# An attention stage whose query blocks are taken in the order 4, 0, 5, 1, 6, 2, 7, 3

## The reference

```python
qb = (q * scale).reshape(b, nb, Q_BLOCK, ATTN_HEADS, 2, ATTN_HEAD_DIM)   # Q_BLOCK = 128, nb = 8
def block(args):                                       # one block of 128 queries, all heads
    q_blk, i = args
    sc = einsum('bhcqd,bhckd->bhcqk', q_blk, kt)       # two maps c per head
    sc = where(k_pos[None, :] <= q_pos[:, None], sc, -inf)
    p = softmax(sc, axis=-1)
    p_diff = p[:, :, 0] - lam * p[:, :, 1]
    return einsum('bhqk,bhkv->bhqv', p_diff, vt)
o = rms_norm(o, subln_g) * (1.0 - lambda_init)
```

## Time and profile before

| | |
|---|---|
| median of 3 runs | 1843.36 us (1842.89 to 1843.89) |
| the profiled execution: its time, its span | 1842.73 us, 1841.1 us |
| PE busy over the span | 1793.0 us, 97% |
| DVE busy over the span | 1137.9 us, 62% |
| the attention, first scores to the last transposes of a difference | 135.5 us to 505 us |

### The profile page before, as it was taken

One profiled execution on the slowest core, in us unless ns is written; L12 is line 12 of the kernel. 1 busy time (PEld: TensorE's weight loads), 2 busy tenths in 40 slices (PEclk: granted clock), 3 DMA queues, 4 the chain that ended last, 5 costly groups with the idle time before them and its releaser, 6 DMA issues. The chain is left out here.

```text
span 1841.1 us, 25124 instructions
## 1 busy us (share of the span) xinstructions
PE 1793.0 (97%) x8628; PEld 1480.4 (80%) x8628; DVE 1137.9 (62%) x1786; ACT 688.4 (37%) x1351; POOL 219.5 (12%) x494
## 2 busy tenths in 40 slices
PE   6999999999999999999999999999999999999997
PEld 5887777777878888888888888888888888788885
DVE  4218888898875774541555645874555555567666
ACT  4216666666644333342221123433333333222122
POOL 2121111111110001112100112100000000000002
PEclk9999999999999999999999999999999999999999
DMA  6220111111132223327635612212222222333332
GB/s 216 92 64 27 55 59 57 58 57 57 46 138 80 76 67 104 126 81 262 217 126 171 229 57 108 86 69 74 97 68 91 80 75 96 103 127 124 125 126 92
DMA packets 123088, 187.11 MB, mean 102 GB/s; under 512 B 5936, under 2 KB 93488, under 8 KB 121984
## 3 DMA queue, kind: packets, MB, share of 16 engines
q1 hardware_dynamic: 99376, 99.36, 17.1%
q0 software_dynamic: 23344, 85.69, 12.7%
q10 hardware_dynamic: 288, 1.05, 0.2%
HBM read 136.79 MB, written 49.28 MB: 101 GB/s over the span
## 5 line engine op out<-in xcount | busy, mean ns | idle before, releaser
L2056 PE MATMUL ps<-w_d,hn 128*128 128x512 f32 x960 | 218.1, 389 | 0.0
L2122 PE MATMUL ps<-xn,ring 128*128 128x512 f32 x864 | 214.2, 398 | 1.4 <-DVE qt L1431 1.0
L2056 PEld LDWEIGHTS ps<-w_d,hn 128*128 128x128 f32 x960 | 180.2, 188 | 37.4
L2122 PEld LDWEIGHTS ps<-xn,ring 128*128 128x128 f32 x864 | 158.3, 189 | 33.1 <-issue 1.1
L2365 PE MATMUL ps<-s_op,t_op_T 128*128 128x512 f32 x720 | 170.0, 389 | 2.2 <-ACT a_copy L786 2.2
L2365 PEld LDWEIGHTS ps<-s_op,t_op_T 128*128 128x128 f32 x720 | 135.1, 188 | 30.7 <-ACT a_copy L786 2.7
L2231 PE MATMUL ps<-s_op,x_op_T 128*128 128x512 f32 x540 | 127.4, 389 | 0.0
L1996 DVE TENSOR_TENSOR ff_sum<-ff_sum,ps 128x512 f32<-128x512 f32 x128 | 87.9, 687 | 52.5 <-PE ps L2056 52.5
L2231 PEld LDWEIGHTS ps<-s_op,x_op_T 128*128 128x128 f32 x540 | 101.4, 188 | 21.0
L2365 PE MATMUL ps<-hn,t_op_B 128*128 128x512 f32 x480 | 115.1, 389 | 0.0
L2365 PEld LDWEIGHTS ps<-hn,t_op_B 128*128 128x128 f32 x480 | 90.1, 188 | 18.7
(11 more groups left out here) (221 smaller groups left out, 3199.1 us busy)
## 6 DMA issues: line engine op xcount, KB each, us to landing
pair<-in_w_gate_up_dram SPq DMA_DIRECT2D x20, 1024.0 KB, 5.1
x_pair<-in_w_in_dram SPq DMA_DIRECT2D x15, 1024.0 KB, 6.4
raw<-in_w_in_dram SPq DMA_DIRECT2D x28, 512.0 KB, 4.0
raw_down<-in_w_down_dram SPq DMA_DIRECT2D x22, 512.0 KB, 3.4
raw_down<-hf_scratch SPq DMA_DIRECT2D x22, 512.0 KB, 3.2
hf_scratch<-hf_out POOLq DMA_DIRECT2D x40, 256.0 KB, 2.3
gate_in<-gate_scratch POOLq DMA_DIRECT2D x18, 512.0 KB, 3.6
y_scratch<-y_out POOLq DMA_DIRECT2D x8, 1024.0 KB, 4.2
```

Of the source, the lines that this page charges most:

```text
L2056: last = pe.matmul(ps[:, bank, :], lhs, rhs, start=i == 0, stop=i == len(pairs) - 1)
L2122: last = pe.matmul(ps[:, proj_bank(first, half), :], ring[:, which, a, P * k:P * (k + 1)], xn[:, b, k, HALF * half:HALF * (half + 1)], sta ...
```

## The change

The block of a step is no longer its index: a table gives it. Large and small blocks alternate.

```diff
+        BLOCKS = (4, 0, 5, 1, 6, 2, 7, 3)
+        def half_of(which, turn):
+            return 1 - turn if which else turn
...
             def exps(i, c):
-                w = P * (i + 1)
+                w = P * (BLOCKS[i] + 1)
...
             def scores(par, i):
                 wait_for(pe, exp_done, t.at() * 2)
-                for chunk in range(i // 4 + 1):
-                    w = min(HALF, P * (i + 1) - HALF * chunk)
+                q = BLOCKS[i]
+                for chunk in range(q // 4 + 1):
+                    w = min(HALF, P * (q + 1) - HALF * chunk)
```

The same replacement is made in `masked`, `maximum`, `difference`, the copies of the transposes, `diff_transposed`, `weighted_values` and `y_lo`/`y_hi`. Since block 4 comes first, the second half of the queries is projected first (`half_of(1, turn)` is `1 - turn`), in the prelude of head 0 as well:

```diff
             def proj_part(which, part, first=False):
-                half, ks = part // 2, range(4 * (part % 2), 4 * (part % 2) + 4)
+                half, ks = half_of(which, part // 2), range(4 * (part % 2), 4 * (part % 2) + 4)
+                bank = proj_bank(first, part // 2)
...
                     if i == 0:
                         pe.wait_ge(proj_lo, p.at(-1))
-                    if i == 4:
-                        pe.wait_ge(proj_lo, p.at(-2))
+                    if i == 1:
+                        pe.wait_ge(proj_lo, p.at())
                     scores(par, i)
```

The two weight splits of a head move one step up, on ACT and on DVE; the split of the values stays at the fifth step:

```diff
                 if not lag:
-                    if i in (2, 6):
+                    if i in (1, 5):
                         split_next()
                     if i == 4 and not last:
                         split_v(1 - par)
                     if i % 2 == 1 and not last:
-                        proj_lo_of(1 - par, i // 4, i // 2 % 2)
+                        proj_lo_of(1 - par, i // 4, half_of(i // 4, i // 2 % 2))
```

More of the change, by code:

```diff
@@ L859, in _, with proj_hi_of @@
             t, heads_in, heads_out = Count(), Count(), Count()
-            def proj_hi_of(par, which, half, first=False):
+            def proj_hi_of(par, which, half, first=False, turn=None):
                 act.wait_ge(proj_done, p.at(1))
-                copy((kt, qt)[which][:, par, HH, HALF * half:HALF * (half + 1)], ps[:, proj_bank(first, half), :],
+                bank = proj_bank(first, half if turn is None else turn)
+                copy((kt, qt)[which][:, par, HH, HALF * half:HALF * (half + 1)], ps[:, bank, :],
                      scale=(1.0, HD ** -0.5)[which]).then_inc(proj_hi, 1)
@@ L931, in y_hi @@
                     act.wait_ge(y_free, heads_out.at())
-                transposed_hi(1, y_out[:, par, HH, P * i:P * (i + 1)].rearrange("p (k t) -> p k t", t=P), 1)
+                s = slice(P * BLOCKS[i], P * BLOCKS[i] + P)
+                transposed_hi(1, y_out[:, par, HH, s].rearrange("p (k t) -> p k t", t=P), 1)
             def split_v(par):
@@ L946, in step_of @@
                     before = (i - 1) % TT
-                    for b in range(before // 4 + 1):
-                        blocks = min(4, before + 1 - 4 * b)
+                    for b in range(BLOCKS[before] // 4 + 1):
+                        blocks = min(4, BLOCKS[before] + 1 - 4 * b)
                         transposed_hi(b, pt[:, before % 2, HH, 4 * b:4 * b + blocks, :], blocks)
@@ L978, in _ @@
             for half in range(2):
-                proj_hi_of(0, 1, half, first=True)
+                proj_hi_of(0, 1, half_of(1, half), first=True, turn=half)
             for i in range(TT):
@@ L1426, in _, with proj_lo_of @@
             t = Count()
-            def proj_lo_of(par, which, half, first=False):
+            def proj_lo_of(par, which, half, first=False, turn=None):
                 dve.wait_ge(proj_hi, p.at(1))
                 buf, s = (kt, qt)[which], slice(HALF * half, HALF * (half + 1))
-                dve.scalar_tensor_tensor(buf[:, par, LL, s], ps[:, proj_bank(first, half), :], (1.0, HD ** -0.5)[which],
+                dve.scalar_tensor_tensor(buf[:, par, LL, s], ps[:, proj_bank(first, half if turn is None else turn), :],
+                                         (1.0, HD ** -0.5)[which],
                                          buf[:, par, HH, s].bitcast(F32), ALU.mult, ALU.subtract)\
@@ L1455, in masked @@
                 dve.wait_ge(scores_done, t.at(1))
-                block = ps[:, i // 4:i // 4 + 3:2, P * (i % 4):P * (i % 4 + 1)]
+                q = BLOCKS[i]
+                block = ps[:, q // 4:q // 4 + 3:2, P * (q % 4):P * (q % 4 + 1)]
                 did(dve.tensor_tensor(block, block, mask[:, :, :], ALU.add))
@@ L1477, in y_lo @@
             def y_lo(par, i):
-                transposed_lo(1, lambda s: y_out[:, par, s, P * i:P * (i + 1)].rearrange("p (k t) -> p k t", t=P), 1)
+                cols = slice(P * BLOCKS[i], P * BLOCKS[i] + P)
+                transposed_lo(1, lambda s: y_out[:, par, s, cols].rearrange("p (k t) -> p k t", t=P), 1)
             def step_of(par, i, lag=0, first=False, last=False):
@@ L1513, in _ @@
             for half in range(2):
-                proj_lo_of(0, 1, half, first=True)
+                proj_lo_of(0, 1, half_of(1, half), first=True, turn=half)
             dve.wait_ge(mask_ready, 2)
@@ L2121, in proj_part @@
                     for a, b in PASSES:
-                        last = pe.matmul(ps[:, proj_bank(first, half), :], ring[:, which, a, P * k:P * (k + 1)],
+                        last = pe.matmul(ps[:, bank, :], ring[:, which, a, P * k:P * (k + 1)],
                                          xn[:, b, k, HALF * half:HALF * (half + 1)],
@@ L2137, in scores @@
                             rows = slice(HD * c, HD * (c + 1))
-                            last = pe.matmul(ps[:, 2 * c + chunk, 0:w], qt[rows, par, a, P * i:P * (i + 1)],
+                            last = pe.matmul(ps[:, 2 * c + chunk, 0:w], qt[rows, par, a, P * q:P * (q + 1)],
                                              kt[rows, par, b, HALF * chunk:HALF * chunk + w],
@@ L2144, in diff_transposed @@
                 pe.wait_ge(diff_ready, t.at())
-                for b in range(i // 4 + 1):
-                    blocks = min(4, i + 1 - 4 * b)
+                for b in range(BLOCKS[i] // 4 + 1):
+                    blocks = min(4, BLOCKS[i] + 1 - 4 * b)
                     transpose_rows(b, diff[:, i % 2, HALF * b:HALF * b + P * blocks], blocks)
@@ L2153, in weighted_values @@
                     heads_v.next()
-                for b in range(i // 4 + 1):
+                for b in range(BLOCKS[i] // 4 + 1):
                     pe.wait_ge(tr_free[b], tr[b].at(-newer[b]))
                 wait_for(pe, u_ready, t.at(-2))
-                for k in range(i + 1):
+                for k in range(BLOCKS[i] + 1):
                     pe.matmul(ps[:, U_BANK, 0:2 * HV], pt[:, i % 2, HH, k, :], vh[:, par, :, k, :],
-                              start=k == 0, stop=k == i, skip_group_check=True)
+                              start=k == 0, stop=k == BLOCKS[i], skip_group_check=True)
                     last = pe.matmul(ps[:, U_BANK, 0:HV], pt[:, i % 2, LL, k, :], vh[:, par, HH, k, :],
-                                     start=False, stop=k == i, skip_group_check=True)
+                                     start=False, stop=k == BLOCKS[i], skip_group_check=True)
                 last.then_inc(pv_done, 1)
@@ L2181, in step_of @@
                     diff_transposed(before)
-                    newer = (1, before // 4)
+                    newer = (1, BLOCKS[before] // 4)
                 if lag == 1:
```

11 lines of the change are left out of this document (6 added, 5 removed).

## The result

| | kernel before | changed kernel |
|---|---|---|
| median | 1843.34 us (1841.91 to 1844.84, 7 runs) | 1848.96 us (1846.97 to 1851.17, 7 runs) |
| ratio, 95% interval | | 1.0031, 1.002 to 1.0042 |
| profiled execution: time, span | 1842.73, 1841.1 | 1847.28, 1845.7 |
| head 0 | 42.04 | 44.36 |
| loop, six heads in all | 279.85 | 284.54 |

The change makes the kernel slower by 0.31%, 5.6 us. The prediction said 1846.3 us, +0.16%. The range (1840.5 to 1850.5) holds the result, and so does the forecast's own (1843.5 to 1849), by 0.04 us; "within 0.2%", which the prediction gave as its likeliest case, does not.

A forecast was written before the change was run, and what follows sets the result against it. PE is busy 97% of the span, so only its idle time in the attention, mostly waits for DVE, can move. Loop +2.6, head 0 +2.7, head 7 and end -2.4 give +2.9 us: 1846.3 us, range 1840.5 to 1850.5.

The forecast's parts named there:

- within 0.2%: Whole kernel: the forecast's case, a steady head of 46.8 to 47.2 us and a time within 0.2%; chance 0.47.
- The ring: One steady attention head, followed along whatever ends last: eight stretches summing to 46.97 us, against 46.64 before.
- S1 to M2: From the start of block 0's scores to block 5's mask: 6.46 us, DVE's side adding up to 6.5.
- the bank in step 5: PE's wait for bank 5 behind block 6's first four transposes: 1.05 us, where the kernel before has 0.56.
- the last difference: Last head's end: PE's wait for block 3's difference, 1.03 us before, would fall to 0.3.
- waits at `rsums`: Sign of being wrong: the forecast fails if waits stand at `rsums`; no size given.
- The loop's turn: DVE's next mask 1.50 us late, 1.3 absorbed by block 4's step; 0.2 us left in three of six heads.
- Head 0 and the end: First head, nothing covering block 4's chain: +2.7 us; head 7 and the end: -2.4 us.
- Rival 1: Step 5, block 6's copy on DVE needing ACT's: exponentials 0.5 us later, +3.8, 1850 us; chance 0.37 with its neighbours.
- M5 to M6: From block 2's mask to block 7's mask on DVE: 6.30 us, much other would show the prediction wrong.
- Rival 2: Large blocks' chain is DVE's own work, short copies shorten it: 1.8 us a head, 1834 us; faster cases together 0.16.
- Rival 3: Spread over a head, DVE's work fits under PE's: 2.3 us a head, 1830 us; faster cases together 0.16.

The follow-up runs named there:

- c3: Changed kernel with ACT's high half of the values' split in step 3 and DVE's low half ahead of step 4's difference: 1842.98 us, 1.0003 of the kernel before.
- b4: Changed kernel with the weight splits put back in steps 2 and 6, block order as changed: 1858.53 us, 1.0086 of the kernel before.
- a3: Changed kernel with DVE's low half of the values' split issued behind step 4's `y_lo`: 1845.96 us, 1.0016 of the kernel before.
- a2: Changed kernel with DVE's loop over heads 1 to 6 written out, other engines' loops kept: 1845.82 us, 1.0016 of the kernel before.
- d1: Kernel before with the values' split moved to step 0 of the head that uses them, POOL's load left in place: 1836.38 us, 0.9964.
- a1_again: The changed kernel measured once more, no edit: 1847.77 us, 1.0027 of the kernel before.
- b2: Kernel before with the values' split in step 0 and POOL's load behind step 3's norm, loops kept: 1836.36 us, 0.9961.
- c1: Kernel before with the weight splits in steps 1 and 5, block order as before: 1843.69 us, 0.9999.
- b1: Changed kernel with the values' split in step 0, POOL's load behind step 3's norm and DVE's loop written out: 1838.4 us, 0.9971 of the kernel before.
- a4: Changed kernel with the values' split in step 0 of the head that uses them, POOL's load left in place: 1849.42 us, 1.0037 of the kernel before.
- c2: Kernel before with only POOL's load moved behind step 3's norm, the values' split left in step 4: 1882.33 us, 1.0203.
- b3: Kernel before with the values' split in step 0, POOL's load behind step 3's norm and DVE's loop written out: 1837.24 us, 0.9961.

## Why the prediction was right, and where it was not

**The ring: right.** Steady heads are 46.95 us against 46.97 forecast, and no stretch is off by more than 0.04. The chains that the prediction named (exponentials for a large block, norm for a small one, the values' split in front of bank 5) are the ones in the trace, and c3 and b4 move the heads by what these chains give. In S1 to M2 some of that is luck: DVE's side adds up to 6.5, the prediction took 6.46 without a reason, and 6.43 came.

The waits' sizes came less well: 0.80 for the bank in step 5 against 1.05 (the split starts at 349.11 and PE goes on at 350.78, 1.67 us later as said, but the four transposes in front end, by their record, at 349.98 and cover 0.87 of it, not 0.6), about 0.15 for the last difference against 0.3 (its transposes start 0.37 us behind the `y_row` transpose at 507.37, where 0.22 is usual); the differences' 0.25 to 0.68 and the norm's 0.28 to 0.56 are near what was said (0.2 to 0.8, 0.4 to 0.7), the one of 0.28 in step 5 being below it. a3 shows a coupling that the ring had left out: what delays `sum_u` delays the norm of the next step.

One of the signs of being wrong did appear: waits at `rsums`, 28 of them, 15.8 us in all. By the prediction's own account of the order (a short copy behind a large block leaves DVE waiting for the exponentials) they had to appear. The ring had priced the stretches from a large block's mask to its difference whole, exponentials included, so their lengths held (5.02 against 5.00, 6.01 against 6.02). The sign was listed wrongly; the ring does not fall with it.

**The loop's turn: mis-sized, and the cause of the miss.** The prediction carried the 1.50 us of the earlier trace rows over as a delay of fixed length, gave block 4's step 1.3 us of room for it, and so left "0.2 us in three of six heads". Measured: the odd heads of a2, whose DVE has no turn, are 0.18 us longer than the even ones (so were those of the kernel before, 46.78 against 46.51; whose doing that is stays open; in the old order it goes when the values' split moves, d1). On top of these 47.13 us the turn costs 1.17 and 1.10 us in heads 3 and 5 of the first trace, 1.24 and 1.40 in a1_again, and nothing in head 1, which stands behind the loop's entry. The six heads together: 6 x (46.95 - 46.64) + 3 x 0.18 + 2.3 = +4.7 us, where the prediction had 2.0 + 0.6 = +2.6. The room was right: of gaps of 2.42, 2.35, 2.40 and 2.60 us on DVE (two turns in each of the two traces) 1.25, 1.25, 1.16 and 1.20 do not reach the head's length. The gap was wrong, because it is not of fixed length. In ACT's timeline, first before, then after, the high copy of `y_out` is the last thing that DVE waited for ahead of the turn:

```profile
270.98 0.28 ACT L786 ACTIVATE y_out<-ps 128x128 fp32r<-128x128 f32 x1
```

```profile
272.41 0.28 ACT L792 ACTIVATE y_out<-ps 128x128 fp32r<-128x128 f32 x1
```

From its end to DVE's next mask it is 274.33 - 271.26 = 3.07 us before and 275.76 - 272.69 = 3.07 after. In the old order DVE is behind and still has 1.5 us of work in hand when that wait is released, so only 1.50 shows, and step 0 absorbs it. In the new one DVE has caught up: 2.42 shows, of which block 4's chain absorbs about half. The rest arrives at PE in step 1:

```profile
278.88 0.55 PE L2151 MATMUL ps<-kt,qt 64*128 64x128 f32 x6 [0.16 <-ACT e_t L911]
...
280.39 0.76 PE L2075 MATMUL ps<-ident,diff 128*128 128x128 f32 x5 [0.95 <-DVE diff L1459]
```

That the turn is the cause is shown (a2). That its length counts from the last wait passed is read from eleven traces, not tried by an experiment, and what DVE's sequencer does in that time no run shows.

The Trainium skill (Advanced Engine Details and Errata, Control Flow Timing) gives a compare-and-branch about 108 ns; no row here shows a single branch. The turn of this loop costs far more than one: the same way, from ACT's copy to DVE's mask, takes 0.82 us in head 4, where there is no turn, so the turn adds 2.25 us, about 21 times that figure.

**Head 0 and the end: right in kind.** Head 0 +2.32 against +2.7; block 4's transposes wait 0.77 us for the difference in step 1, where 0.85 was said. The end -2.98 against -2.4: head 7 to its last difference's transposes takes 507.74 - 462.65 = 45.09 us (forecast 45.1 to 45.4) and the short steps behind it have a little less. The attention as a whole is then +2.32 + 4.69 - 2.98 = +4.0 us instead of +2.9.

**The rest is not shown to be the change's.** The first scores come 1.7 us earlier (133.75 against 135.47). Over the traces of all kernels here they come between 133.75 and 135.47 in no order, so this is chance. Against it stands +2.3 us behind the attention, +1.9 of it in one place of the feed-forward. PE waits there for ACT about as long as before, and in the trace of before the granted clock stays at 1.00. In that of after it falls: 12 matmuls run at the lower level, 1.2 GHz, for part of the stretch.

```profile
1583.34 3.02 PE L2365 MATMUL ps<-s_op,t_op_T 128*128 128x512 f32 x12 [2.23 <-ACT a_copy L786]
```

```profile
1586.23 4.61 PE L2378 MATMUL ps<-s_op,t_op_T 128*128 128x512 f32 x12 [2.53 <-ACT a_copy L792]
```

In b2, which has the old order, the same 12 matmuls take 4.54 us after a wait of 2.57, and c1, old order too, shows a clock of 0.97 over the same 50 us as the changed kernel. In fact the trace of before is the only one of fourteen without this fall: in the other thirteen, five of them of the old order, the 12 matmuls take 4.33 to 4.61 us after waits of 2.01 to 2.68. So the order is not needed for it; why the first trace was spared is open. From the attention's end to the span's, the six traces of the old order take 1312.1 to 1314.5 us, the eight of the new one 1312.4 to 1314.7. A hint the other way stays unexplained: the mean granted clock is 0.995 or 0.996 in all 15 runs of the changed kernel, and 0.996 or 0.997 in 62 of the 63 runs of the kernel before that were taken beside the experiments. The falls may thus be more frequent in the new order.

In the profiled runs the parts add up: -1.7 + 4.0 + 2.3 = +4.6 us of span. The medians differ by 5.6, and the interval (3.7 to 7.7 us) holds both; of these 5.6 the attention's 4.0 are placed, the other 1.6 are not. With the turn taken out, a2 stands 2.8 us above the kernel before, where the prediction had +2.9 with only 0.6 for the turn.

**The rivals.** Rival 1 (slower, 1850, for a delay of block 6's copy on DVE by ACT in step 5) came nearer in time, 1.0 us off where the forecast was 2.7 off, but by the wrong mechanism: no wait for ACT's copy stands there, and M5 to M6 is 6.27. A reader who had gone by the time alone would have believed it. Rival 2 (short copies shorten the chain) falls: DVE waits for the exponentials 28 times. Rival 3 (DVE fits under PE) falls with the 26 waits for a difference. The unasked question was the larger one: not in which order the blocks stand, but where the values' split stands. Its move is worth 1.0 us a head in the old order (b2, d1) and, with the load moved behind a norm, 0.9 to 1.1 in the new (b1 against a2); the best version keeps the old order.

## What to carry to other kernels

When an engine that is nearly saturated holds a buffer that others wait for, first move the work that stands between its last use and its release, and only then think of the order of the blocks; a filler belongs where that engine waits for another (c3: -0.69 us a head, b2: -1.0). Price a loop's turn from the last wait passed ahead of it (read from the traces here, not tried), not from the gap that the old profile shows: a change that lets the engine catch up uncovers it. A load and the work that its wait is tied to are one step; moved singly, either can block a queue (a4: DVE's wait for the norm rises from 0.56 to 1.54 us) or starve the split (c2: +39 us).

## What the hardware showed unexpectedly

- In the eleven traces with DVE's loop kept, old order and new, two turns each, DVE's first instruction behind the turn started 2.99 to 3.27 us after the end of the ACT copy that DVE had last waited for. At the head's start in the middle of the unrolled pair, with DVE just as caught up, it is 0.82 us, of which 0.15 is a wait for the scores (head 4); with the loop written out (a2) it is 0.82 at the turn's place too.
- The turn can be hidden whole: in the old order heads 3 and 5 (46.78 us) are as long as head 1 (46.77), and writing the loop out gives nothing (b3).
- A wait of PE of 2.0 to 2.7 us in the feed-forward was followed by a fall of the granted clock in thirteen traces (0.79 over 1584 to 1592 us in the changed kernel) and not in one (1.00 in the kernel before, after 2.23 us); 12 matmuls then took 4.3 to 4.6 us instead of 3.0. In a4 it also fell behind two shorter waits, 0.96 and 0.81 us.
- POOL's issue of one load takes 0.95 or 0.98 us, where the norm's own instructions take 0.18 to 0.56.
